# Six products of constants per layer, mixed into the norm sums ahead of the gated memory

## The chip, the core and the metric

One core of a Trainium2 chip runs the whole program. The metric is device microseconds of one execution, and its median over the runs. TensorE (PE) multiplies matrices into PSUM, VectorE (DVE), ScalarE (ACT) and GpSimd (POOL) work on tiles, and SyncE (SP) issues the loads.

## What is computed

Two blocks of two layers each on 512 tokens of width 1024, in fp32. The change lies in the second block, whose layer is, cut to what matters:

```python
for l in range(2):
    h = rmsnorm(x, norm1_g[l])
    u = h @ w_in[l]                    # split into the inputs of three mixers
    y_m = mlstm_mixer(...)             # gated memory: 4 heads of 64, a norm at its end
    y_a = diff_attention(...)          # 4 heads of 128, rmsnorm over each head of the output
    y_h = hgrn2_mixer(...)             # 4 heads of 64, rmsnorm over each head of the output
    x = x + concat([y_m, y_a, y_h]) @ w_out[l]
    x = x + square(relu(rmsnorm(x, norm2_g[l]) @ w_up[l])) @ w_down[l]
```

The norms in question are those of the outputs of `diff_attention` and `hgrn2_mixer`: each needs the mean square of a head for every token.

## The kernel before

Every engine has one instruction stream, written out in order; semaphores tie the streams together. Tensors lie with features on 128 partitions and the 512 tokens in the free dimension, in four blocks of 128 tokens. Large products run in three fp32r passes (high and low parts of both operands, `u_hi`, `u_lo`, `w_hi`, `w_lo`) into the PSUM banks `LP[0]` and `LP[1]`; smaller work uses the four banks `XB[0]` to `XB[3]`. In plain fp32 every product shows as two records in the trace.

In the second block each layer runs the input products, then `diff_attention` (line 736) unit by unit with `beside_maps` (line 1167) slipping other work between the units, then the stretch of the change, lines 1231 to 1246. There TensorE:

- waits for four squared tiles (`mix_squared`), and takes the column sums of six tiles of squares with `mix_sum` (line 1208): the squares are the stationary operand, a column or two of constants the moving one, so a product has one or two columns. The two tiles `tabs` of the recurrence come first (two columns, 8 products, 16 records), then three tiles `wk` of the attention heads (one column, 12 products, 24 records);
- waits for the attention's output to be copied out (`o_taken`), computes the second scores of the gated memory (`memory_scores(1)`, line 1152) and its first weighted values (`weighted(0)`, line 1193);
- sums the last attention head's squares, which releases ScalarE's square root (`mix_summed`);
- goes on with scores and weighted values, and from the fourth step on spreads the reciprocal roots over partitions (`mix_spread`, line 1218), which releases VectorE's scaling of the mixed outputs (line 2843).

VectorE in the same stretch multiplies scores with gates (`memory_weights`, line 2811), and cuts the low parts of the output weights and of the mixed tensor (lines 2084 and 2092). The output products `wo` begin as soon as the mixed tensor's chunks are cut.

`fill(n, bank)` (line 630) is a helper that is in use already: n products of the identity with 256 columns of a table of constants (`causal`), whose result nobody reads. `fill_heads` puts such products between the units of the attention, and `total_sum` and `spread` (lines 641 and 665) put them into the norms of the first block when called with `filled=4`: two behind the first four sums, two behind the last, four behind the spread. The late norms (`late_norm`, line 701) call both without any. Their sums sit inside the first slab of the product that needs the norm (line 605), ahead of its last pass.

Of the kernel before, what the change touches and what calls it, by code (L numbers as in the profile page):

```python
# [188 lines left out]
def build(nc, x, small, consts, consts2, pos, adab, w, out):  # L189
    with ExitStack() as ctx:  # L190
        sems = {}

        def s(name):
            if name not in sems:
                sems[name] = ctx.enter_context(nc.semaphore(name))
            return sems[name]
# [61 lines left out]
        XB = [XBS[:, i, :] for i in range(4)]  # L258
# [57 lines left out]
        def cc(name, a=0, n=None):  # L316
            t, (o, wd) = (cst, COFF[name]) if name in COFF else (cst2, COFF2[name])
            return t[:, o + a:o + (wd if n is None else a + n)]
# [39 lines left out]
        def blk(b):  # L358
            return slice(b * P, (b + 1) * P)
# [25 lines left out]
        for l in range(DEPTH):  # L385
            ORDER += [(f"in{l}", 11, DC * 256, 0, 1), (f"inv{l}", 4, DC * 256, 0, 1), (f"wo{l}", 4, DC * 256, 0, 1)]
            for part in "ab":
                ORDER += [(f"up{l}{part}", 8, DC * 256, 0, 1), (f"down{l}{part}", DC, 16 * P, 0, 1)]
        WIDTH = {name: (n, width, ada) for name, n, width, ada, _ in ORDER}
        CUT = {name for name, _, _, _, two in ORDER if two}  # L390

        CUT_SLABS, HIGH_HOME, slabs = [], [], 0
        HIGH_CHUNKS = {"hybo": (FK, FV), "mlao": (0, KN), "wo0": (AQ, AK, HQ, XQ), "wo1": (AQ, AK, HQ, XQ)}
        for name, n, width, _, two in ORDER:
            CUT_SLABS += [(slabs + k, width) for k in range(n if two else 0)]
            homes = HIGH_CHUNKS.get(name, ())
            HIGH_HOME += [(homes[k % len(homes)],) if homes else () for k in range(n if two else 0)]
            slabs += n

        BESIDE = [name in HIGH_CHUNKS and k < 2 for name, n, _, _, two in ORDER for k in range(n if two else 0)]  # L400

        def wo_cuts(q):
# [131 lines left out]
        def _(pe):  # L534
            pl = Place(pe, s)

            def mm(o, lhsT, rhs, start=True, stop=True):
                return pe.matmul(o, lhsT=lhsT, rhs=rhs, start=start, stop=stop)  # L538
# [91 lines left out]
            def fill(n, bank=XB[3]):  # L630

                for _ in range(n):
                    mm(bank[:, 0:256], cc("ident"), cc("causal", 0, 256))
# [394 lines left out]
            for l in range(DEPTH):  # L1028
# [123 lines left out]
                def memory_scores(n):  # L1152

                    cp, b = memory_step(n)
                    if n >= 2:
                        pe.wait_ge(s("ms_ready"), u0 + n - 1)
                    for j in range(2):
                        last = mm(LP[(n + 1) % 2][:, j, 0:T - b * P], big[half(j), XK + cp, blk(b)],
                                  big[half(j), XQ + cp, b * P:T])
                    last.then_inc(s("mqk_done"), 1)  # L1160
# [47 lines left out]
                def mix_sum(i, square):  # L1208

                    for b in range(NB):  # L1210
                        o = 8 * b + i
                        if i < DIFF_H:
                            last = mm(XB[3][:, o:o + 1], square[:, blk(b)], cc("ones", 0, 1))
                        else:
                            last = mm(XB[3][:, o:o + 2], square[:, blk(b)], selw[:, 6:8])
                    return last
# [12 lines left out]
                    last.then_inc(s("mix_spread"), 1)  # L1229

                pl.got("mix_squared", 4)
                for cp in range(2):
                    mix_sum(4 + 2 * cp, tabs[:, cp, :])
                for hh in range(3):
                    mix_sum(hh, wk[:, hh, :])
                pe.wait_ge(s("o_taken"), pl.head)
                memory_scores(1)
                weighted(0)
# [1841 lines left out]
```

## Time and profile before

| | us |
|---|---|
| median of 3 runs | 3507.31 |
| lowest, highest | 3507.28, 3509.19 |
| the profiled execution | 3506.33 |
| its span of instructions | 3504.5 |
| TensorE busy in it | 3436.8 |
| VectorE, ScalarE, GpSimd busy | 1478.0, 1021.9, 1527.5 |

A row of the timeline gives the start from the span's start, the time from the first start to the last end of merged instructions, the engine, the line, the operation, out<-in with shapes, and the count. The end of a matmul is modelled, so rows of TensorE overlap by some 0.1 us. The chain of waits goes back from the last instruction, at each step to what released it; the time of its pieces adds up to the span.
### The profile page before, as it was taken

What the parts mean: (1) busy time and instruction counts of PE and PEld (TensorE: products, weight loads), DVE (VectorE), ACT (ScalarE), POOL (GpSimd) and SP (SyncE); (2) the same over time, 40 slices, a digit from 0 to 9 for tenths busy, and PEclk for the clock granted to TensorE, in tenths of its full rate; (3) what the DMA queues carried; (4) which work ended last, traced back from release to release, by engine and by line L of the source; (5) the groups of instructions that cost most, each with busy time, mean ns of one, the idle gap of its engine ahead of it and who ended that gap; (6) DMA issues with size and microseconds to landing.
All of it is one profiled execution on the core that took longest, in us unless ns stands there. A gap on an engine that the chain in (4) does not pass through costs nothing.

```text
span 3504.5 us, 42095 instructions
## 1 busy us (share of the span) xinstructions
PE 3436.8 (98%) x16800; PEld 2762.3 (79%) x16800; DVE 1478.0 (42%) x2571; ACT 1021.9 (29%) x1275; POOL 1527.5 (44%) x524
## 2 busy tenths in 40 slices
PE   7999999899999999999999999999999999999999
PEld 6878878588888888886888886877888868778887
DVE  6565268855253524146412126854101168641010
ACT  2222322632123222224222233443212234342221
POOL 3545552035455545540354554502646545125463
PEclk9999999899999999999999999999999999999999
DMA  6435322025343444211223222201222222012222
GB/s 258 187 144 202 101 84 73 1 86 203 125 185 121 179 151 153 95 51 65 73 85 113 85 95 69 83 25 49 96 96 96 96 72 76 34 49 85 97 99 79
DMA packets 54877, 360.70 MB, mean 103 GB/s; under 512 B 6080, under 2 KB 6464, under 8 KB 17728
## 3 DMA queue, kind: packets, MB, share of 16 engines
q1 hardware_dynamic: 54720, 358.53, 28.4%
q8 instruction: 108, 1.77, 0.2%
q14 instruction: 49, 0.40, 0.0%
HBM read 356.41 MB, written 2.10 MB: 102 GB/s over the span
## 4 chain that ended last, share of the span: by engine, by line
PE 92%; DVE 4%; ACT 1%; issue 1%; POOL 1%; DMA 1%; SPq 0%; DVEq 0%; POOLq 0%; ACTq 0%
PE LP L538 82%; PE XB L538 8%; ACT E L1312 1%; POOL w_lo L1812 1%; PE LP L911 1%; DMA big<-w_ada 1%; DVE wk L2099 1%; PE XB L757 0%; DVE XB L2025 0%; PE XB L793 0%; ACT sq L1312 0%; DVE big L2209 0%; DVE big L2208 0%; DVE h L2287 0%; DVE S L2370 0%
## 5 line engine op out<-in xcount | busy, mean ns | idle before, releaser
L1812 POOL TENSOR_TENSOR w_lo<-ring,w_hi 128x2048 fp32r<-128x2048 f32 (+3 forms) x277 | 1147.1, 4142 | 808.4 <-ACT w_hi L1312 808.1
L538 PE MATMUL LP<-u_hi,w_hi 128*128 128x512 f32 x2480 | 972.2, 392 | 11.4 <-ACT u_hi L1312 6.0
L538 PE MATMUL LP<-u_hi,w_lo 128*128 128x512 f32 x2480 | 966.1, 390 | 0.0
L538 PE MATMUL LP<-u_lo,w_hi 128*128 128x512 f32 x2480 | 942.7, 390 | 0.0
L538 PE MATMUL LP<-big_r,w_hi 128*128 128x512 f32 x2520 | 780.1, 390 | 3.9 <-POOL w_lo L1812 3.2
L1312 ACT ACTIVATE w_hi<-ring 128x2048 fp32r<-128x2048 f32 (+3 forms) x277 | 478.6, 1728 | 900.6 <-PE LP L538 743.7
L538 PE MATMUL LP<-big_r,w_lo 128*128 128x512 f32 x1508 | 587.5, 390 | 0.0
L538 PEld LDWEIGHTS LP<-u_hi,w_hi 128*128 128x128 f32 x2480 | 466.1, 188 | 127.6 <-issue 26.4
L538 PEld LDWEIGHTS LP<-big_r,w_hi 128*128 128x128 f32 x2520 | 472.8, 188 | 104.2 <-issue 4.1
L538 PEld LDWEIGHTS LP<-u_hi,w_lo 128*128 128x128 f32 x2480 | 466.2, 188 | 97.3
L538 PEld LDWEIGHTS LP<-u_lo,w_hi 128*128 128x128 f32 x2480 | 466.4, 188 | 96.0 <-issue 0.5
L1849 POOL TENSOR_TENSOR big_r<-tmp,big_r 128x512 f32 (+2 forms) x120 | 192.5, 1605 | 577.6 <-DVE big_r L2183 416.2
L538 PEld LDWEIGHTS LP<-big_r,w_lo 128*128 128x128 f32 x1508 | 283.4, 188 | 58.7
L2188 DVE TENSOR_TENSOR tmp<-tmp,LP 128x512 f32<-128x512 f32 x88 | 60.5, 687 | 543.5 <-ACT tmp L1312 533.3
L2025 DVE SCALAR_TENSOR_TENSOR XB<-ada_in,csil,XB 128x256 f32<-128x256 f32 x460 | 225.2, 490 | 16.1
L1312 ACT ACTIVATE tmp<-LP 128x512 f32<-128x512 f32 x89 | 53.2, 598 | 603.0 <-PE LP L538 603.0
L1812 POOL TENSOR_TENSOR w_lo<-ring,big_r 128x2048 fp32r<-128x2048 f32 x8 | 36.7, 4587 | 440.5 <-ACT big_r L1312 440.5
L2264 DVE SCALAR_TENSOR_TENSOR h<-LP,gate,h 128x512 f32 (+1 forms) x64 | 48.0, 751 | 350.3 <-PE LP L538 349.8
L2902 DVE TENSOR_TENSOR h<-h,LP 128x512 f32 x32 | 22.0, 687 | 317.0 <-PE LP L538 317.0
L2896 DVE SCALAR_TENSOR_TENSOR tmp<-LP,tabs 128x1024 f32<-128x1024 f32 x32 | 39.2, 1224 | 237.1 <-PE LP L538 237.1
L1312 ACT ACTIVATE E<-S,stat 128x128 f32<-128x128 f32 (+3 forms) x160 | 88.7, 555 | 135.6 <-DVE stat L2373 42.3
L538 PE MATMUL XB<-big 64*128 64x128 f32 (+5 forms) x472 | 111.6, 460 | 0.0
(335 smaller groups left out, 3510.9 us busy)
## 6 DMA issues: line engine op xcount, KB each, us to landing
ada_in<-w_ada SPq DMA_DIRECT2D x66, 1024.0 KB, 4.9
ring<-w_in SPq DMA_DIRECT2D x22, 1024.0 KB, 4.8
ring<-w_gu00a SPq DMA_DIRECT2D x11, 1024.0 KB, 7.0
ring<-w_gu00b SPq DMA_DIRECT2D x11, 1024.0 KB, 6.7
ring<-w_gu01a SPq DMA_DIRECT2D x11, 1024.0 KB, 6.6
ring<-w_gu01b SPq DMA_DIRECT2D x11, 1024.0 KB, 6.6
ring<-w_gu10a SPq DMA_DIRECT2D x11, 1024.0 KB, 6.7
ring<-w_gu10b SPq DMA_DIRECT2D x11, 1024.0 KB, 6.9
```

The source lines that it names most:

```text
L538: return pe.matmul(o, lhsT=lhsT, rhs=rhs, start=start, stop=stop)
L911: last = pe.transpose(LP[1][:, j, blk(b)], E[:, 2 * (k % 2) + j, blk(b)], cc("ident"))
L1312: return act.activation(o, i, fn, **kw)
L1812: gp.tensor_tensor(w_lo[:, slab % RING, 0:width], ring[:, slab % RING, 0:width], w_high(q, width).bitcast(F32), ALU.subtract).then_inc(s(" ...
L1849: gp.tensor_tensor(big_r[:, lo, :], src, big_r[:, hi, :].bitcast(F32), ALU.subtract)\
L2025: ins = stt(ada_acc[:, :] if c == DC - 1 and a < UP0 else part, wv[:, c * 256:(c + 1) * 256], csil[:, c:c + 1], part, ALU.mult, ALU.add)
L2099: tt(o, o, square_home(c, late), ALU.add).then_inc(s("sq_added"), 1)
L2188: tt(o, tmp[:, p, 0:T].unsqueeze(1), LP[p][:, 1:2, :], ALU.mult))
L2264: stt(o, LP[p][:, 0:1, :], g, o, ALU.mult, ALU.add).then_inc(s(f"lin_taken{p}"), 1)
L2896: stt(o, LP[p][:, :, :], 0.0, over_two(R), ALU.max, ALU.mult).then_inc(s(f"lin_taken{p}"), 1)
L2902: tt(o, o, LP[p][:, 0:1, :], ALU.add).then_inc(s(f"lin_taken{p}"), 1)
```

## The change

Three calls of `fill` are added between the sums, into bank `XB[0]`. Nothing else differs.

```diff
                 pl.got("mix_squared", 4)
+                fill(1, XB[0])
                 for cp in range(2):
                     mix_sum(4 + 2 * cp, tabs[:, cp, :])
+                fill(2, XB[0])
                 for hh in range(3):
                     mix_sum(hh, wk[:, hh, :])
+                fill(3, XB[0])
                 pe.wait_ge(s("o_taken"), pl.head)
                 memory_scores(1)
                 weighted(0)
```

The helper that they call:

```python
def fill(n, bank=XB[3]):
    for _ in range(n):
        mm(bank[:, 0:256], cc("ident"), cc("causal", 0, 256))
```

Each layer of the second block thus gets six more products of 256 columns, twelve in all (24 records). The first 256 columns of `causal` are zero.

## Rows read from the trace of the kernel before

**Rows 1.** The page: TensorE's busy time, and the chain that ended last by engine.
```profile
PE 3436.8 (98%) x16800; PEld 2762.3 (79%) x16800; DVE 1478.0 (42%) x2571; ACT 1021.9 (29%) x1275; POOL 1527.5 (44%) x524
...
PE 92%; DVE 4%; ACT 1%; issue 1%; POOL 1%; DMA 1%; SPq 0%; DVEq 0%; POOLq 0%; ACTq 0%
```

**Rows 2.** The chain of waits, layer 0: start us, us, what.
```profile
2361.56 4.77 PE XB L538 x40
2366.33 2.00 PE LP L538 x4
2368.34 4.79 PE XB L538 x16
...
2373.97 1.99 PE XB L538 x8
...
2387.21 0.44 DVE u L2843
```

**Rows 3.** Stretches, layer 0: us, busy PE PEld DVE ACT POOL, PEclk, DMA, GB/s.
```profile
2364.00:2366.00 2.00, 2.00 (x18) 2.00 (x17) 0.00 (x0) 1.98 (x3) 0.00 (x0) 0.83 0.00 0
...
2370.00:2372.00 2.00, 2.00 (x6) 0.19 (x4) 0.62 (x2) 0.00 (x0) 0.00 (x0) 0.50 0.00 0
2372.00:2374.00 2.00, 2.00 (x16) 1.42 (x16) 0.00 (x0) 0.82 (x2) 0.00 (x0) 0.96 0.00 0
```

**Rows 4.** The timeline of TensorE in the same stretch.
```profile
2361.40 1.84 PE L538 MATMUL XB<-ada_in,tabs 128*128 128x2 f32 x16
2363.10 3.23 PE L538 MATMUL XB<-cst,wk 128*128 128x1 f32 x24
...
2368.27 1.97 PE L538 MATMUL XB<-S,big 128*64 128x512 f32 x4
...
2372.02 1.10 PE L538 MATMUL XB<-cst,tabs 128*128 128x1 f32 x8
```

**Rows 5.** The chain of waits, layer 1: first weighted values and last sum.
```profile
3074.76 4.85 PE XB L538 x16
```

**Rows 6.** Stretches elsewhere: layer 1's, two norms of block one, two late norms.
```profile
3072.00:3078.00 6.00, 6.00 (x16) 1.65 (x16) 2.16 (x3) 0.79 (x1) 0.00 (x0) 0.50 0.00 0
...
1713.00:1714.00 1.00, 1.00 (x8) 1.00 (x9) 0.00 (x0) 0.00 (x0) 0.00 (x0) 0.70 1.06 442
...
1121.00:1123.00 2.00, 2.00 (x15) 1.65 (x15) 2.00 (x2) 0.63 (x1) 2.00 (x1) 1.00 0.00 0
...
2451.00:2454.00 3.00, 3.00 (x21) 2.72 (x22) 0.18 (x1) 0.26 (x1) 0.00 (x0) 1.00 0.00 0
...
2095.00:2097.00 2.00, 2.00 (x8) 1.59 (x7) 0.84 (x5) 0.30 (x1) 0.00 (x0) 0.67 0.00 0
```

**Rows 7.** The timeline of TensorE: three and five fill products between attention units.
```profile
2345.68 1.56 PE L538 MATMUL LP<-cst 128*128 128x256 f32 x6
...
2353.44 2.43 PE L538 MATMUL LP<-cst 128*128 128x256 f32 x10 [0.21 <-DVE u L2323]
```

**Rows 8.** The timeline of TensorE: a norm with fills whose clock fell.
```profile
1710.42 1.02 PE L538 MATMUL XB<-cst,wk 128*128 128x1 f32 x8 [0.40 <-DVEq L2108]
1711.31 1.11 PE L538 MATMUL XB<-cst 128*128 128x256 f32 x4
1712.49 2.77 PE L538 MATMUL XB<-cst,sq 128*128 128x1 f32 x16
1715.12 2.05 PE L538 MATMUL XB<-cst 128*128 128x256 f32 x4
```

**Rows 9.** The timeline of TensorE: second sums of a norm whose clock held.
```profile
1122.41 1.05 PE L538 MATMUL XB<-cst,sq 128*128 128x1 f32 x8
```

**Rows 10.** The timeline of TensorE: the late norm of layer 0.
```profile
2450.51 1.93 PE L538 MATMUL XB<-cst,sq 128*128 128x1 f32 x16
2452.29 3.88 PE L538 MATMUL LP<-u_lo,w_hi 128*128 128x512 f32 x16
```

**Rows 11.** The timeline of TensorE: the late norm whose clock fell.
```profile
2094.54 5.49 PE L538 MATMUL LP<-u_lo,w_hi 128*128 128x512 f32 x16
```

## The prediction

> **What bounds the kernel now.** I read the page first. TensorE is busy in 98% of the span and makes up 92% of the chain that ended last [rows 1]; whatever adds time to TensorE's stream, or takes it away, is the time of the kernel, unless another engine is late at that place. So I went to the place of the change with the chain of waits in order of time. In layer 0 the 40 small products of the norm sums (ten sums of four blocks, less the one that comes later, each product being two records) take 4.77 us, the next memory scores 2.00 us and the first weighted values with the last sum 4.79 us, all on TensorE without a wait between; the next values, of the same shape, take 1.99 us. The first other engine on the chain is VectorE at 2387.21 [rows 2]. From 2361.56 to there TensorE alone sets the pace, so a microsecond added in front of the scores arrives whole at 2387.21, and VectorE's serial chain behind it starts that much later.
>
> The granted clock tells why like work costs twice as much. It is whole until some 2365.3 (0.83 as the mean of 2364 to 2366), 0.50, the level of 1.2 GHz, until about 2372.2, and back at 2.4 GHz after (0.96 as the mean of 2372 to 2374) [rows 3]. TensorE is busy without a gap all this time (2.00 of 2.00 us); what it did before the fall is one- and two-column sums, from 2361.40 on [rows 4]. Layer 1 has the same shape, 4.85 us for the same values and 0.50 from 3072 to 3078 [rows 5, 6]. So there is a real loss to win back.
>
> **What the change costs.** It moves and removes nothing. It adds six products of 256 columns to each layer: one ahead of the sixteen records of two columns, two behind them, three behind the 24 records of one column, all before the wait ahead of the scores. The same products stand elsewhere in the kernel: three (6 records) take 1.56 us and five (10 records) 2.43 us, at whole clock [rows 7], so one more costs (2.43 - 1.56) / 2 = 0.43 us. At half clock I take twice that, 0.85 us; two of them at 0.50 took 2.05 us as a group against 1.11 us at whole clock [rows 8]. Six are 2.6 us at whole clock and 5.1 us at half. Their bank, XB[0], has its last reader far behind and its next writer (the first values) starts its bank afresh, so no wait comes with them; they read constants only. Nothing hides them, since the engine has no gap here [rows 3]. Behind them on TensorE are the scores and all weighted values; VectorE and ScalarE wait for those already (their chains go through TensorE up to 2387.21), so no other engine becomes late.
>
> **What the change can give.** The first values start at 2368.27 and the last sum at 2372.02 [rows 4]: 3.75 us at half clock, where the next ones of the same shape take 1.99 us [rows 2]. That is 1.76 us, and the scores are worth half of their 2.00 us, 1.0 us more. If the clock never fell, a layer would have 2.6 - 1.76 - 1.0 = -0.2 us. So even complete success is nearly nothing. The sums themselves gain nothing: 24 records take the same some 0.13 us each on both sides of the fall.
>
> **Does the clock fall all the same?** The nearest row is a norm of this very kernel: eight records of sums, two such fill products, sixteen records of sums, two fills [rows 8]. The clock fell inside its second sums (0.70 as the mean of 1713 to 1714) and the fills behind them ran at half clock [rows 6]. The same norm with eight records behind the first two fills kept its clock, 1.00 from 1121 to 1123 [rows 6, 9]. The change leaves 24 records of sums unbroken, a longer run than the sixteen with which the clock fell, behind two fills as there. So I take it to fall within the second run of sums, near the same moment, 2365.3.
>
> The sum of layer 0 then: fill 0.43, two fills 0.85, the sums 4.77 as before, three fills at half clock 2.56: the scores start at 2361.56 + 8.61 = 2370.2 and end, at half clock, at 2372.2. If the clock is low for as long as now, it is back at that moment, and the first values run at whole clock: 1.76 us less. New 4.77 + 0.43 + 0.85 + 2.56 + 2.00 + (4.79 - 1.76) = 13.64 us, old 11.56 us: +2.1 us. Bounds for one layer: -0.2 us (never falls), and 5.1 us if all six are at half clock and nothing is gained behind them; the rows lie near the fall in mid-sums, so +2.1. Layer 1 repeats it: **+4.2 us** for both, though its fall may lie elsewhere in the sums by then.
>
> The Trainium skill, "TensorE: Matmul & The Clock Gate", Part 1, says that the clock is low by default and that activity releases it; by that alone the added products would hold it, and the sum would be -0.4 us. The trace has both outcomes for sums with fills among them, so the rule doesn't settle it.
>
> **A second effect, through the placement of later work.** 24 records of sums without a fill stand in the late norm behind layer 0, at 2450 [rows 10], and the clock held: 1.00 from 2451 to 2454 [rows 6]. In the norm of rows 8 24 records with two fills among them lost it. So content alone doesn't decide; where a stretch begins does too, and the change shifts all later stretches. Three places past layer 0's sums hold their clock now and have few columns: this late norm, its twin in layer 1, and the start of layer 1's attention. What a fall costs is in the late norm where it fell (mean 0.67 from 2095 to 2097 [rows 6]): sixteen large products took 5.49 us [rows 11] against 3.88 us at whole clock [rows 10], **+1.6 us**, all of it on TensorE's path. The start that the shift gives each place is not in the trace; I take each near even, so one or two of three would fall, and count one: 1.6 us. The same page's section says that the gate's watching runs free of the kernel; that agrees with like stretches faring differently here, and gives no price.
>
> **The rivals.** (1) *Further places lose the clock.* The mechanism is that shift, its places are the late norms at 2450 and 3156, the price is 1.6 us each and more than one must go: 4.2 + 3.2 = 7.4 us, 3514.7; with the attention start too, 9.0 us, 3516.3. For it: their neighbours of like content fell. Against it: they may shift to a start that holds. This is the one that ends slower than a measurement's doubt. (2) *The clock falls at the sums, nothing later falls:* +4.2 us, 3511.5. (3) *The clock holds in both layers:* -0.4 us, 3506.9; one layer only +1.9 us. For it: the added products put full columns into three places of the stretch, and the norm at 1121 held. Against it: the unbroken 24 records. (4) *The clock falls and stays low longer, or falls at the start of the fills:* up to 3.8 us a layer with nothing gained behind, 7.7 us, 3515.0, more with a later fall.
>
> **How the numbers follow.** Forecast: both fall, one later place falls, 4.2 + 1.6 = +5.8 us. The profiled execution took 3506.33 us (span 3504.5), 1.0 below the median of 3507.31; the runs shown reach 3509.19. The sum is a difference, so I put it on the median: **3513.1 us**. Chances: this 0.34; rival 1 0.29; rival 2 0.17; rival 3 0.12, with one or both layers holding; rival 4 0.08. Low end 3508.5: rival 2 and most of one layer holding are in, both holding is out. High end 3517.5: rival 1 with all three is in. A measurement of this kernel can tell about 0.2%, 7.0 us, from no change. Only rival 1 (most of it) and rival 4 pass 7.0 us: slower 0.37. Faster by 7.0 us has no mechanism here: 0.02. Within it 0.61.
>
> **What would show it.** In the profile after: at the sums a clock of 0.50 beginning in the 24 one-column records or behind them; the three fills at about 0.85 us each; the first values at 2 to 3 us instead of 3.75; the same chain with no other engine before the end of the mixer's weighted values. The clock at 2450 and 3156, shifted, tells of the second effect: sixteen products at 3.9 us or at 5.5 us. I am wrong if the clock is 1.00 through both stretches, if VectorE takes up the added time between 2387 and 2392, or if clock changes ahead of layer 0's sums, which the change doesn't touch, make up the difference.

## The result, and the profile after

| | before | changed |
|---|---|---|
| median of 18 runs, us | 3509.09 | 3515.65 |
| lowest, highest | 3505.3, 3521.02 | 3511.41, 3526.59 |
| the profiled execution | 3506.33 | 3515.23 |
| its span | 3504.5 | 3513.4 |

The two medians lie 6.6 us apart. The ratio that all 36 runs give together, and on which I go, is 1.0015, with a 95% interval from 1.0008 to 1.0021: +5.3 us, from +2.8 to +7.4. That is within the 0.2% that the prediction called no change. Repeated later beside another set of runs it was 1.0004 (0.9995 to 1.0013). Weighting the two by the inverse squares of their intervals gives 1.0011 (1.0006 to 1.0017), **+3.9 us**. One thing is plain only now that there are 18 runs of each: single executions of one and the same kernel lie 15 us apart, and the first three of before (3507.28 to 3509.19) made it look far steadier. Most of this scatter lies ahead of the change: the twelve executions profiled for this document run the same program up to layer 0's sums and reach them at 2358.2 to 2370.1 us.

The page after: TensorE's busy time has grown by 9.8 us, and no other engine's has moved by more than 0.1.

```profile
PE 3446.6 (98%) x16824; PEld 2771.9 (79%) x16824; DVE 1478.0 (42%) x2571; ACT 1022.0 (29%) x1275; POOL 1527.5 (43%) x524
...
PE 91%; DVE 4%; ACT 1%; issue 1%; POOL 1%; DMA 1%; SPq 0%; DVEq 0%; POOLq 0%; ACTq 0%
```

The chain of waits after, layer 0, where rows 2 are those of before: sums with the six products (52 records), second scores, first values with the last sum, then, after a few more pieces, VectorE as before.

```profile
2360.45 9.95 PE XB L538 x52
2370.40 1.44 PE LP L538 x4
2371.84 2.97 PE XB L538 x16
2374.81 0.85 PE LP L538 x4
...
2388.89 0.44 DVE u L2846
```

The timeline of TensorE there, which answers to rows 4:

```profile
2360.28 0.60 PE L538 MATMUL XB<-cst 128*128 128x256 f32 x2
2360.72 1.84 PE L538 MATMUL XB<-ada_in,tabs 128*128 128x2 f32 x16
2362.42 1.11 PE L538 MATMUL XB<-cst 128*128 128x256 f32 x4
2363.37 4.26 PE L538 MATMUL XB<-cst,wk 128*128 128x1 f32 x24
2367.49 2.91 PE L538 MATMUL XB<-cst 128*128 128x256 f32 x6
2370.33 1.51 PE L538 MATMUL LP<-big 64*128 64x512 f32 x4
```

And stretches of the changed kernel (columns as in rows 3): layer 0's sums and what follows, then layer 1's attention start and its late norm.

```profile
2364.00:2366.00 2.00, 2.00 (x13) 2.00 (x13) 0.00 (x0) 1.19 (x1) 0.00 (x0) 0.58 0.00 0
2366.00:2371.00 5.00, 5.00 (x16) 3.82 (x18) 0.00 (x0) 0.00 (x0) 0.00 (x0) 0.50 0.00 0
2371.00:2373.00 2.00, 2.00 (x10) 0.34 (x8) 1.04 (x1) 0.00 (x0) 0.00 (x0) 0.97 0.00 0
...
3023.00:3029.00 6.00, 5.25 (x21) 3.55 (x22) 2.79 (x9) 1.37 (x5) 0.00 (x0) 0.51 0.00 0
3166.00:3169.00 3.00, 3.00 (x10) 2.40 (x11) 0.18 (x1) 0.26 (x1) 0.00 (x0) 0.57 0.00 0
```

The clock fell all the same, a little after 2364, while TensorE was busy without a gap, as forecast; the three products behind the sums ran at half clock (2.91 us for six records). It is back before 2371.2, so the first values run at whole clock. I call **a stretch** the time from the first sum (or product ahead of it) to the third scores, which in the chain is the sum of the three pieces. Before it is 4.77 + 2.00 + 4.79 = 11.6 us [rows 2], after 9.95 + 1.44 + 2.97 = 14.4 us. Layer 1's is 14.4 too. So the two profiles say +2.8 us a layer, 5.6 of the 8.9 us between the spans. The rest is in layer 1: its attention's start at a clock of 0.51, and its late norm at 0.57. These are the chain's pieces at the attention's start and the sixteen large products behind the late norm's sums, each first in the kernel before and then in the changed one:

```profile
3022.07 1.13 PE LP L538 x8
3026.87 5.55 PE LP L538 x60
...
3023.75 2.08 PE LP L538 x8
3031.38 5.55 PE LP L538 x60
...
3158.76 3.88 PE L538 MATMUL LP<-u_lo,w_hi 128*128 128x512 f32 x16
...
3166.07 5.50 PE L538 MATMUL LP<-u_lo,w_hi 128*128 128x512 f32 x16
```

The attention's start took 7.6 us where it had taken 4.8 (+2.8), and the sixteen products 1.6 us more. Together with the stretches that would be 10.0 us; against it stands 1.1 us by which this execution reached the place of the change earlier (2360.45 for 2361.56), which the change has no part in.

### The profile page after: what moved, and what is told of

Read it like the earlier page. It is cut to its first block, busy times and chain, and to the rows that moved or that the text cites. A ratio compares the mean times of both kernels' runs of the same rounds, so it can differ in the third digit from the quotient of the medians.

```text
span 3513.4 us, 42143 instructions
## 1 busy us (share of the span) xinstructions
PE 3446.6 (98%) x16824; PEld 2771.9 (79%) x16824; DVE 1478.0 (42%) x2571; ACT 1022.0 (29%) x1275; POOL 1527.5 (43%) x524
## 4 chain that ended last, share of the span: by engine, by line
PE 91%; DVE 4%; ACT 1%; issue 1%; POOL 1%; DMA 1%; SPq 0%; DVEq 0%; POOLq 0%; ACTq 0%
PE LP L538 82%; PE XB L538 8%; POOL w_lo L1815 1%; ACT E L1315 1%; PE LP L911 1%; DMA big<-w_ada 1%; DVE wk L2102 1%; PE XB L757 0%; DVE XB L2028 0%; PE XB L793 0%; ACT sq L1315 0%; DVE big L2212 0%; DVE big L2211 0%; DVE h L2290 0%; DVE S L2373 0%
```

## The experiments

Ratios are to the kernel before on the same chip, with their 95% intervals.

**The products in layer 0 alone.**

```diff
+                f0 = 1 - l
                 pl.got("mix_squared", 4)
+                fill(f0, XB[0])
                 for cp in range(2):
                     mix_sum(4 + 2 * cp, tabs[:, cp, :])
+                fill(2 * f0, XB[0])
                 for hh in range(3):
                     mix_sum(hh, wk[:, hh, :])
+                fill(3 * f0, XB[0])
```

> The added products stand in layer 0 alone. Theory A (each product costs its time at the granted clock, and the clock falls all the same): layer 0's stretch, from the first sum to the second scores, takes about 14.4 us as in the changed kernel (11.6 before), layer 1's stays near 11.6, and the median moves by about +2.8 us, half of the whole change's. Theory B (what was measured comes mostly from later places that lose their clock by the shift): the median moves as much as with both layers, 5 us or more, though only 2.8 us are in the stretch.

Measured: 1.0012 (1.0001 to 1.0022), +4.2 us from 0.4 to 7.7: too wide to part the theories. The profile was worth more. Layer 0's stretch took 12.7 us, not 14.4, and layer 1's, which has no product and the program of before, 10.0, not 11.6:

```profile
3076.17 4.36 PE XB L538 x40
3080.53 1.28 PE LP L538 x4
3081.81 4.35 PE XB L538 x16
```

Both misses have one reason: the clock fell later than in the first profiles. In layer 1 all forty records of the sums ran at whole clock, 4.36 us, and the low clock lay behind them, on the scores and the start of the values (0.54 as the mean of 3081 to 3084, then 1.00 from 3085 to 3087). A stretch of one and the same program does not have one length. Behind the products this profile lost time at the same two later places as the changed kernel's first: the clock is 0.50 from 3027 to 3033, at the attention's start, and from 3167 to 3170, in the late norm.

**Twelve products, two around every eight records.**

```diff
                 pl.got("mix_squared", 4)
+                fill(2, XB[0])
                 for cp in range(2):
                     mix_sum(4 + 2 * cp, tabs[:, cp, :])
+                    fill(2, XB[0])
                 for hh in range(3):
                     mix_sum(hh, wk[:, hh, :])
+                    fill(2, XB[0])
```

> Two products ahead of and behind every eight records of sums, twelve a layer instead of six. Theory A (the clock falls because the one-column sums stand unbroken, and no fixed number of products between them is a cure unless they stand close enough): the clock stays at 1.00 through both stretches; twelve products cost 12 x 0.43 = 5.1 us, the scores and first values give back 1.0 + 1.8 us, so a stretch takes 11.6 + 5.1 - 2.8 = 13.9 us and the kernel is about 4.6 us slower, less than the fills of the change cost per product. Rival (products of constants with zeros as the moving operand don't hold the clock at all): the clock falls here too, and a stretch takes 17 us or more, the kernel 11 us slower.

Measured: 1.0015 (1.0003 to 1.0026), +5.3 us. The clock held in both layers, and both stretches took 9.65 + 1.06 + 2.97 = 13.7 us:

```profile
2361.00:2375.00 14.00, 14.00 (x89) 10.65 (x87) 3.33 (x6) 4.27 (x7) 0.00 (x0) 1.00 0.00 1
3073.00:3087.00 14.00, 14.00 (x87) 10.65 (x88) 3.33 (x6) 4.25 (x8) 0.00 (x0) 1.00 0.00 0
```

So such products do hold the clock, though their moving operand is all zeros, once they stand close enough; the rival falls. They pay for it in full: twelve of them that hold the clock cost the kernel about what six do that don't. Its timeline also gives the price of a group of eight sums at whole clock: 0.81 us, from 2365.52 to the next group at 2366.33.

```profile
2365.52 0.95 PE L538 MATMUL XB<-cst,wk 128*128 128x1 f32 x8
2366.33 1.11 PE L538 MATMUL XB<-cst 128*128 128x256 f32 x4
```

**All six behind the sums.**

```diff
                     mix_sum(hh, wk[:, hh, :])
+                fill(6, XB[0])
                 pe.wait_ge(s("o_taken"), pl.head)
```

> All six products of a layer stand behind the sums, ahead of the scores. Theory A: the sums run at whole clock until the same fall as before, some 3.8 us in; the six then run at half clock until it returns. If it returns 3.4 us after the fall, the rest, the scores and the values run at whole clock: stretch near 4.8 + 4.3 + 1.1 + 2.0 + 0.9 = 13.1 us, +1.5 us a layer. If it stays low 6.8 us as before: near 4.8 + 5.1 + 1.5 + 2.0 + 0.9 = 14.3 us, +2.7 us a layer. Theory B gives the same as the changed kernel for the whole, as the added time is alike.

Measured: 1.0022 (1.0012 to 1.0032), +7.7 us. Layer 0's stretch took 12.8 us, layer 1's 16.0 us. In layer 0 the sums ran at whole clock, the 24 records from 2359.75 to 2362.44, which is 0.11 us each:

```profile
2359.75 2.83 PE L538 MATMUL XB<-cst,wk 128*128 128x1 f32 x24
2362.44 4.50 PE L538 MATMUL XB<-cst 128*128 128x256 f32 x12
```

In layer 1 the clock fell early:

```profile
3072.06 4.96 PE L538 MATMUL XB<-cst,wk 128*128 128x1 f32 x24
3076.88 5.47 PE L538 MATMUL XB<-cst 128*128 128x256 f32 x12
...
3073.00:3082.00 9.00, 9.00 (x31) 7.73 (x31) 0.00 (x0) 2.24 (x3) 0.00 (x0) 0.50 0.00 0
```

All six products ran at half clock, and so did nearly all of the 24 records: 4.82 us from 3072.06 to 3076.88, a mean of 0.20 us. The records start 0.11 us apart for the first 0.3 us and 0.21 us apart from there on, twice the time of whole clock. That is a term that the prediction had wrong (below).

**Real work between the sums instead of products.** Scores and values, which must be computed anyway, are put between sums of eight records; `weighted` takes a function that it calls between its values and its column sums. ScalarE takes the root one step later (`n == 3` for `n == 2`).

```diff
-                for cp in range(2):
-                    mix_sum(4 + 2 * cp, tabs[:, cp, :])
-                for hh in range(3):
-                    mix_sum(hh, wk[:, hh, :])
+                mix_sum(4, tabs[:, 0, :])
                 pe.wait_ge(s("o_taken"), pl.head)
                 memory_scores(1)
+                mix_sum(6, tabs[:, 1, :])
                 weighted(0)
-                pl.got("mix_squared")
-                mix_sum(3, tabs[:, 2, :]).then_inc(s("mix_summed"), 1)
-                for n in range(2, 2 * NB + 1):
+                mix_sum(0, wk[:, 0, :])
+                memory_scores(2)
+                weighted(1, lambda: mix_sum(1, wk[:, 1, :]))
+                memory_scores(3)
+                mix_sum(2, wk[:, 2, :])
+
+                def last_sum():
+                    pl.got("mix_squared")
+                    mix_sum(3, tabs[:, 2, :]).then_inc(s("mix_summed"), 1)
+
+                weighted(2, last_sum)
+                for n in range(4, 2 * NB + 1):
```

> No product is added. The scores and weighted values that follow the sums are put between them, one sum of eight records at a time, and ScalarE's root is taken one step later. Theory A (the loss is the clock's, and the sums are short enough to leave it whole when full columns stand between them): granted clock 1.00 through both stretches, work of the stretch in the same amount at whole clock, so 2.8 us less a layer: about -5.6 us, 0.9984. Rival (another engine is next: VectorE's products of scores with gates and ScalarE's root come later than the shortened stream of TensorE needs them): the clock holds but TensorE waits 1 to 3 us a layer for them, and the kernel is within 2 us of before.

Measured: 0.9985 (0.9972 to 0.9997), -5.3 us. The clock was whole in both layers:

```profile
2364.00:2379.00 15.00, 15.00 (x93) 8.28 (x91) 7.48 (x14) 7.26 (x12) 0.00 (x0) 1.00 0.00 1
3071.00:3085.00 14.00, 14.00 (x85) 7.47 (x84) 7.17 (x13) 6.29 (x11) 0.00 (x0) 1.00 0.00 1
```

The chain up to the fifth scores is all TensorE's, with no wait of another engine in it:

```profile
2364.51 0.79 PE XB L538 x8
2365.30 1.12 PE LP L538 x4
2366.42 3.96 PE XB L538 x24
2370.38 0.85 PE LP L538 x4
2371.22 2.97 PE XB L538 x16
2374.20 0.85 PE LP L538 x4
2375.04 3.53 PE XB L538 x24
2378.57 0.63 PE LP L538 x4
```

From 2364.51 to 2378.57 is 14.1 us. The same work before, in its first profile, ran from 2361.56 [rows 2] to 2378.38, 16.8 us: 2.8 us less a layer. The rival, VectorE or ScalarE as the next bound, did not come.

> Scores and values between the sums once more, for a narrower interval and a second profile. Theory A: clock 1.00 through both stretches again and 14.1 us from the first sum to the fifth scores (16.8 before), 2.8 us less a layer, 0.9984 to 0.9989 depending on how early the clock came back in the kernel before. Rival (the first profile was a lucky one): the clock falls between the sums in one layer at least, and the median is within 2 us of before.

Measured: 0.9991 (0.9981 to 1.0000), with a clock of 1.00 and the same pieces again (0.79, 1.12 and 3.96 us at 2363.38, 2364.17 and 2365.29, and from 3071.80 on in layer 1). The two together, weighted as above: 0.9989 (0.9981 to 0.9996), -3.9 us, and -5.5 us lies in the interval. So this version beats the kernel before, and by the ratios to that kernel the changed one too. Both profiles gave part of the gain back later. From the fifth scores of layer 0 to layer 1's first sum they took 692.4 and 694.4 us, where two profiles of before took 689.7: the attention's start of layer 1 had a clock of 0.60 (3020 to 3027) and 0.57 (3022 to 3026), and in the second profile the late norm of layer 0 (0.57 from 2452 to 2456) and another piece of the attention (0.57 from 3053 to 3057) fell as well.

**The kernel before and the changed one once more.**

> The kernel before once more, for a second profile. Theory A: the clock falls at other moments of the sums than in the first profile, so that a stretch takes 10.0 us (as layer 1's of the kernel with products in layer 0 alone) to 11.6 us, and late norms or the attention's start may fall in it. Theory B: the same places as in the first profile, 11.6 us in both layers and no fall in the late norms or at the attention's start in layer 1.

The kernel before took 3511.07 us this time, its span being 3509.3. Layer 0's stretch:

```profile
2364.67 6.36 PE XB L538 x40
2371.02 2.00 PE LP L538 x4
2373.03 4.84 PE XB L538 x16
```

That is 13.2 us, not 11.6; the clock's mean was 0.54 from 2366 to 2376, so it fell earlier in the sums and stayed low through scores and values. Layer 1's was 11.6. Neither theory had named 13.2 us. A place of the attention ahead of layer 0's sums lost its clock that had kept it in the first profile:

```profile
2346.00:2349.00 3.00, 3.00 (x13) 1.95 (x12) 2.51 (x13) 2.55 (x7) 0.00 (x0) 0.54 0.00 0
```

But the places that theory B speaks of behind the sums kept it, as in the first profile: 1.00 at the attention's start of layer 1 (3027 to 3033) and in both late norms (2453 to 2458, 3161 to 3165). On this point theory B was right.

> The changed kernel once more, for a second profile. Theory A: the clock falls in or behind the second run of sums in both layers again, and a stretch takes 12.7 to 14.4 us; other later places than in the first profile lose their clock. Theory B: again the attention's start in layer 1 and the late norm in layer 1, and no other.

The changed kernel took 3517.2 us. Its stretches were 8.54 + 1.21 + 2.97 = 12.7 and 8.89 + 2.01 + 3.46 = 14.4 us. The same two later places fell as in its first profile (0.50 from 3025 to 3031, 0.54 from 3168 to 3171), and in addition one in layer 0's attention, ahead of the change (0.50 from 2346 to 2349). Behind the sums theory B was right; theory A's "other places" was not.

**The same six among the output products.**

```diff
                 out_products(1, range(2))
+                fill(6, XB[0])
                 for k in (2, 3):
```

> The kernel before, with the six products of a layer put among the output products instead, where full columns stand on both sides and the clock is whole. They cost 12 x 0.43 = 5.1 us and shift all later work of a layer by 2.6 us, about as the change does. Theory A (a shift has no cost of its own on average; which places lose their clock differs from execution to execution anyway, the kernel before included): +5.1 us, 1.0015, and the stretches of the sums still take 10 to 12 us. Theory B (the kernel before stands at starts that hold its clock, and a shift loses them): two or three more falls of 1.6 us each on top, +8 to +10 us, 1.0025.

Measured: 1.0024 (1.0011 to 1.0037), +8.4 us. The price of the products themselves is as forecast: 12 records in 2.75 us at whole clock.

```profile
2427.72 2.75 PE L538 MATMUL XB<-cst 128*128 128x256 f32 x12
```

The stretches, which have no product in them here, took 4.36 + 1.96 + 3.72 = 10.0 us in layer 0 and 6.40 + 2.01 + 4.79 = 13.2 us in layer 1. The interval holds both theories, so this kernel was measured again beside the changed one.

> The six products among the output products once more, since the first interval (+3.9 to +13.0 us) holds both theories. Theory A (a shift has no cost of its own on average): +5.1 us again, 1.0015, and the interval of this run reaches below 1.0018. Theory B (the shift itself costs): +8 us or more, 1.0023 and above, as in the first run's middle.

Measured: 1.0019 (1.0009 to 1.0029), stretches of 10.0 and 13.2 us. Both runs together: 1.0021 (1.0013 to 1.0029), +7.3 us from 4.6 to 10.1. The 5.1 us of the products lie in it, and so do 8 us. Both profiles took 702.3 us from layer 0's third scores to layer 1's first sum, where before took 694.9: the products are 2.75 us of that, and 4.6 us come on top, in a late norm (0.58 from 2453 to 2457 in the second) and at the attention's start of layer 1 (0.59 from 3023 to 3027) among others. The traces thus speak for theory B, and the medians don't decide.

> The changed kernel beside it on the same chip. Theory A: a stretch of the sums takes 12.7 to 14.4 us in both layers, 2.1 us more than the 11.6 us that the seven profiled stretches without products in them take in the mean; +4.2 us in all, 1.0012, less than for the same products among the output products by the 0.9 us that the clock's earlier return gives back. Theory B: 1.0023 or above, as for the dense ones.

Measured: 1.0004 (0.9995 to 1.0013), +1.4 us, with stretches of 14.4 and 12.7 us. The late norms kept their clock this time, but the attention's start of layer 1 (0.57 from 3025 to 3029) and a later piece of that attention (0.66 from 3055 to 3060) did not. Layer 1's stretch:

```profile
3074.63 8.64 PE XB L538 x52
3083.28 1.10 PE LP L538 x4
3084.38 2.97 PE XB L538 x16
```

**All stretches together**, in us, from the first sum to the third scores:

| the sums with | profiled stretches | mean |
|---|---|---|
| no product | 11.6, 11.6, 13.2, 11.6, 10.0, 10.0, 13.2, 10.0, 13.2 | 11.6 |
| six products as in the change | 14.4, 14.4, 12.7, 14.4, 12.7, 14.4, 12.7 | 13.7 |
| six behind the sums | 12.8, 16.0 | 14.4 |
| twelve, evenly | 13.7, 13.7 | 13.7 |

The first row is from four kernels that share this piece of program (before twice, products in layer 0 alone, products among the output products twice). The difference of the first two means is 2.1 us a layer, 4.1 us for both, and the measured change of the whole is 3.9 us (2.0 to 5.8).

**The rest of the kernel in the same profiles**, in us; a stretch begins and ends as above, and in these kernels no product is added outside the stretches:

| profile | up to layer 0's stretch | between the stretches | behind layer 1's |
|---|---|---|---|
| before, first | 2361.6 | 694.9 | 424.9 |
| before, second | 2364.7 | 694.9 | 424.9 |
| changed, first | 2360.5 | 697.7 | 426.5 |
| changed, second | 2364.2 | 697.6 | 426.6 |
| changed, third | 2362.3 | 698.0 | 424.9 |
| products in layer 0 alone | 2365.7 | 697.7 | 426.5 |

Behind the first sum of layer 0 the three profiles of the change are 7.6 us longer in the mean than the two of before: 3.7 in the stretches, 2.9 between them and 1.1 behind. That is more than the medians allow (at most 5.8), so two and three executions are too few to say what an average one loses at the later places. Either the kernel before loses its clock there too, in executions that were not profiled, or something else in the profiles is not typical; this stays open. What the profiles do show is that later places lost 3.1 to 4.4 us in each of these four profiles with products, and nothing in either profile of before.

## Why the prediction was right, and where not

- **What bounds.** Right. TensorE's stream alone sets the pace from the sums to the first scaling by VectorE, which came at 2388.89 after 28.44 us in the changed profile, against 25.65 us from 2361.56 in that of before: 2.8 us more, as the stretch itself. Nothing was absorbed.
- **The price of a product.** Right: 0.43 us was forecast at whole clock, 12 records took 2.75 us in the dense place, 0.46 a product with the group's tail. At half clock three took 2.91 us, 0.97 each with the tail, where 0.85 was forecast. Six took 5.47 us, so one product more costs (5.47 - 2.91) / 3 = 0.85 us as forecast; the tenth by which the three were dearer is the end of the group, which the forecast left out.
- **The clock falls all the same.** Right, in all seven profiled stretches of the change. The row that it leaned on, the norm with two fills and sixteen records behind them, was the right neighbour [rows 8]. The Trainium skill, "TensorE: Matmul & The Clock Gate", Part 1, has it that activity releases the clock; the evenly spread twelve agree with that. It was not enough to add activity: it had to leave no long run of sums bare, and a run of eight records was short enough.
- **The sum of +2.1 us a layer.** Right as a mean (2.1), by two errors that cancel and one piece of luck. The step "the sums themselves gain nothing, some 0.13 us each on both sides of the fall" failed: a record of the sums takes 0.11 us at whole and 0.21 us at half clock. The 0.13 was the mean over a run of 24 near whose end the clock fell. So the sums behind the fall were 1.0 us dearer in the first profile after (4.12 us from start to start, where I had put 3.16), and if the clock is held a layer gains more than the 2.8 us of the forecast. Against that, the forecast took the scores at half clock, 2.00 us; they took 1.44 us there, and in the three stretches of 12.7 us the clock was back near their start (1.10, 1.21 and 1.33 us). The luck is that what was measured before is not one number: the stretch that I read as 11.6 us is 10.0 to 13.2, and its mean only happens to be 11.6.
- **The same for the held clock.** Rival 3's -0.2 us a layer is too small a gain for six products. With whole clock a bare stretch would be 4.36 + 1.06 + 2.97 = 8.4 us, 3.2 us under the mean of 11.6; six products that held the clock, at (9.65 - 4.36) / 12 = 0.44 us each, would add 2.6, which makes -0.6 us. That is an estimate from these pieces, and no run has it. The twelve that do hold the clock cost 2.1 us.
- **One later place falls, +1.6 us.** That later places fall shows in the traces; count and price were off. In each of the three profiles of the change two places behind layer 0's sums lost their clock that had kept it in both profiles of before, so by the profiles it was rival 1's case, and not the forecast's one place. The late norm's price stands: its sixteen products took 5.50 us where 3.88 is whole clock. The attention's start, which had no price of its own in the forecast (rival 1 put 1.6 us on it), cost 2.8 us in the first profile. Later places together cost 4.4 us there, and 3.1 us in the third profile, the least. The same two fell with products in layer 0 alone, where layer 1's program is that of before; so products nearby are not what takes the clock there. That the shift does is argued, since no run moves the start of these places by itself.
- **Why the number fits all the same.** The first profile is 8.9 us longer, of which 5.8 were forecast. The measured change is 3.9 us with both comparisons, 5.3 with the first. The 4.2 us of the stretches would do by themselves for the 3.9, and the interval's end at 5.8 leaves at most 1.7 us for the later places; the profiles ask for more. So the forecast of 5.8 lies at the upper end of what was measured by a term whose average size no run shows. That it came so close to 5.3 is partly luck.
- **The median shown.** The forecast's base, 3507.31, was 1.8 us under the median of 18 runs. The absolute time, 3513.1, is 2.5 us under 3515.65 mostly for that.

## What to carry to other kernels

Before paying for products that keep the clock, put work between the slow ones that has to be done anyway: here that gave 2.8 us a layer in the traces where the products, six or twelve, lost 2.1. If products of constants must do it, they have to be spread so that no run of one-column work is long (eight records held here, sixteen and 24 did not always), or their time is spent for nothing, and part of it at half clock. And where the clock falls in some executions and not in others, a stretch of one profile is one draw: take several profiles of the same kernel before pricing a change of a tenth of a per cent, and split all of them into the same parts, the untouched ones too: here parts that the change doesn't touch differed by more than the part that it does.

## What the runs showed of the hardware

- Products whose moving operand is zero hold the clock as well: 1.00 through 14 us with eight-record sums between them.
- One-column fp32 sums with a new 128x128 stationary operand each take twice the time at half clock: 0.11 us a record at 2.4 GHz (2.69 us for 24), 0.21 us at 1.2 GHz (4.82 us for 24, the first three of them still at whole clock).
- The clock falls at different points of the same stretch in different executions. The stretch of the kernel before took 10.0, 11.6 or 13.2 us, and whole executions of it 3504.1 to 3522.0 us over all comparisons.
